# A reordered opening, rotary swaps on the sync engine's queue, and the first output panel's chunks among the attention's last steps

## The reference

```python
mk = rms_norm(rms_norm(mem) @ w_kv[:, :256], per head)       # memory keys, both layers
mv = rms_norm(mem) @ w_kv[:, 256:]                           # memory values
h  = rms_norm(x, norm_mix)
z  = h @ w_in_att                                            # keys, queries, memory queries, values
q, k = rope(rms_norm(q, per head)), rope(rms_norm(k, per head))
o  = concat(sink_softmax(q k^T, window 128) v, softmax(qx mk^T) mv)
x  = x + o @ w_out[0]                                        # the output projection
x  = x + relu(rms_norm(x) @ w_up)^2 @ w_down                 # MLP, then layer 1 in the same way
```

## Time and profile before

| | |
|---|---|
| time, median of 3 runs | 1163.68 us (1163.21 to 1164.44) |
| the profiled execution's own time | 1165.16 us |
| its span | 1163.4 us |
| mean granted TensorE clock | 0.996 of 2.4 GHz |
| TensorE matmuls busy | 1143.0 us, 98% of the span |
| VectorE, ScalarE, GpSimd busy | 781.8, 533.0, 130.4 us |

### The profile page before, as it was taken

How to read it: one execution, slowest core, us unless ns; L and a number is a source line. 1 busy time by engine, 2 the same in 40 slices (tenths; PEclk the granted TensorE clock), 3 DMA queues, 4 the chain that set the end, 5 groups by cost and what they waited for, 6 DMA issues and landing times.

```text
span 1163.4 us, 22291 instructions
## 1 busy us (share of the span) xinstructions
PE 1143.0 (98%) x9026; PEld 1103.2 (95%) x9026; DVE 781.8 (67%) x1215; ACT 533.0 (46%) x920; POOL 130.4 (11%) x143
## 2 busy tenths in 40 slices
PE   7999999999999999999999999999999999999998
PEld 7899646999999999999999999999999999999998
DVE  5857776798568468568657545689866856756853
ACT  6743886367137227326434222436713722732630
POOL 0018853000000000000240131200000000000000
PEclk8999999999999999999999999999999999999999
DMA  8553231213313222312522321221321331231241
GB/s 309 203 162 119 61 139 61 92 59 124 107 39 112 106 72 102 115 51 94 214 75 73 146 82 66 73 100 56 135 99 48 110 109 72 91 125 43 102 137 48
DMA packets 23866, 120.18 MB, mean 103 GB/s; under 512 B 2788, under 2 KB 7012, under 8 KB 10740
## 3 DMA queue, kind: packets, MB, share of 16 engines
q1 hardware_dynamic: 18612, 100.93, 24.8%
q0 software_dynamic: 1632, 10.54, 2.4%
q10 hardware_dynamic: 3552, 7.74, 2.0%
HBM read 111.29 MB, written 5.69 MB: 101 GB/s over the span
## 4 chain that ended last, share of the span: by engine, by line
PE 88%; DVE 3%; POOL 3%; ACT 2%; issue 2%; DMA 1%; ACTq 1%; SPq 0%; DVEq 0%; POOLq 0%
PE zps L507 48%; PE zps L801 25%; PE ops L801 4%; PE zps L789 4%; POOL sm L1955 2%; PE ops L699 1%; PE tps L671 1%; ACTq L1750 1%; PE zps L545 1%; PE zps L625 1%; ACT w_hi L1445 1%; DMA memx<-memT 1%; DMA tmp<-z 1%; ACT act_hi L1445 0%; DVE sm L1090 0%
## 5 line engine op out<-in xcount | busy, mean ns | idle before, releaser
L507 PE MATMUL zps<-act_hi,w_hi 128*128 128x272 f32 x1664 | 349.2, 291 | 0.0
L507 PE MATMUL zps<-act_hi,w_lo 128*128 128x272 f32 x1664 | 344.3, 288 | 0.0
L507 PE MATMUL zps<-act_lo,w_hi 128*128 128x272 f32 x1664 | 343.5, 288 | 0.0
L801 PE MATMUL zps<-xf,wf 128*128 128x272 f32 x2304 | 297.0, 288 | 0.0
L801 PEld LDWEIGHTS zps<-xf,wf 128*128 128x128 f32 x2304 | 292.2, 188 | 0.8
L507 PEld LDWEIGHTS zps<-act_hi,w_hi 128*128 128x128 f32 x1664 | 262.6, 189 | 4.4 <-issue 2.9
L507 PEld LDWEIGHTS zps<-act_lo,w_hi 128*128 128x128 f32 x1664 | 261.9, 189 | 0.0
L507 PEld LDWEIGHTS zps<-act_hi,w_lo 128*128 128x128 f32 x1664 | 260.1, 189 | 0.0
L1445 ACT ACTIVATE w_hi<-w_stage 128x2048 fp32r<-128x2048 f32 (+2 forms) x65 | 115.6, 1779 | 161.6 <-PE zps L507 122.8
L952 DVE TENSOR_TENSOR w_lo<-w_stage,w_hi 128x2048 fp32r<-128x2048 f32 x57 | 133.4, 2341 | 50.9 <-ACT w_hi L1445 50.6
L1445 ACT ACTIVATE wf<-w_sum 128x1024 fp32r<-128x1024 f32 x64 | 68.0, 1062 | 195.4 <-DVE w_sum L970 90.7
(11 more groups left out here) (193 smaller groups left out, 1279.9 us busy)
## 6 DMA issues: line engine op xcount, KB each, us to landing
w_stage<-wst SPq DMA_DIRECT2D x91, 1024.0 KB, 4.9
kx<-xkT POOLq DMA_DIRECT2D x4, 1024.0 KB, 8.5
vx<-xv POOLq DMA_DIRECT2D x4, 1024.0 KB, 7.4
x_res<-xT ACTq DMA_DIRECT2D x2, 1088.0 KB, 8.3
tmp<-z ACTq DMA_DIRECT2D x32, 68.0 KB, 2.1
yT<-x_res ACTq DMA_DIRECT2D x7, 272.0 KB, 2.0
memx<-memT SPq DMA_DIRECT2D x4, 256.0 KB, 5.2
w_stage<-wst SPq DMA_DIRECT2D x4, 256.0 KB, 5.4
```

What stands on the lines that cost most here:

```text
L507: mm = pe.matmul(zps[slot][:, h, 0:n], w_[:, d, k, w:w + 128], r_[:, k, c0 + h * n:c0 + (h + 1) * n], start=(j == 0 and i == 0), stop=(j = ...
L801: mm = pe.matmul(bank, wf_hl[pw][:, fw, a, :], x_form(l, px, fx, a)[:, 0, :], start=(begin and a == 0 and j == 0), stop=(a == KC // 2 - 1 ...
```

## The change

On ScalarE and VectorE the opening's instructions stand in another order. The first weight half of the memory's second column block is loaded in two DMAs with their own semaphores. The column sum stands after chunk 1 of panel 1, the last two turn_keys one panel later. The rotary swaps move from ScalarE's queue to SP's, among the weight loads, which are written out for it. Row 7 is rotated by VectorE; GpSimd rotates seven rows and clears its query tiles afterwards. In the attention VectorE makes the low parts of step J_SS + 1 before a pair's maxima. Panel 0 of the output projection is cut into its chunks: five stand in loop steps 14 to 16 of the attention, three after it.

```diff
 SP
-            sp.dma_start(stage[:, 1], wst[1]).then_inc(w_in[1], 16)
+            for h in range(2):
+                c = slice(4 * h, 4 * h + 4)
+                sp.dma_start(stage[:, 1, c], wst[1, :, c]).then_inc(w_in[1] if h else ld["w3"], 16)
...
             sp.dma_start(o_vs.rearrange("b s d -> s b d"), vb[ST:128, :, :]).then_inc(win_out, 16)
-            weights(Q_ATT + 2, Q_OUT0 + 1)
+            swapped(0)
+            weight(Q_ATT + 2, 0)
+            swapped(1)
+            swapped(2)
+            weight(Q_ATT + 2, 1)
+            swapped(3)
+            swapped(4)
+            weight(Q_OUT0, 0)
+            swapped(5)
+            swapped(6)
+            swapped(7)
+            weight(Q_OUT0, 1)
 TensorE
-                    pe.wait_ge(r_out, 5 if j == 0 else 8)
+                    pe.wait_ge(r_out, 5 if j == 0 else 7)
+                    if j:
+                        pe.wait_ge(r_last, 1)
...
+            def out_chunk(k):
+                if k == 0:
+                    pe.wait_ge(w_los[0], Q_OUT0 + 1)
+                    pe.wait_ge(z_free[0], Q_OUT0 * 2)
+                    pe.wait_ge(g_max, PAIR0[G_L1])
+                pe.wait_ge(g_olo, O0_READY[k])
+                hi, lo = act_hl[0]
+                for i, (w_, r_) in enumerate(((w_hi, hi), (w_hi, lo), (w_lo, hi))):
+                    for h in range(2):
+                        mm = pe.matmul(zps[0][:, h, 0:HALF], w_[:, 0, k, 0:128], r_[:, k, h * HALF:(h + 1) * HALF],
+                                       start=(k == 0 and i == 0), stop=(k == KC - 1 and i == 2))
+                if k == KC - 1:
+                    mm.then_inc(z_full[0], 1)
             def attention_0():
                 for j in range(1, G_L1 + 3):
                     for p in range(3):
+                        if j >= G_L1 and p < (2, 2, 1)[j - G_L1]:
+                            out_chunk(2 * (j - G_L1) + p)
...
-                panel(Q_ATT + i // 4, i % 4, *act_hl[0], ready=normed(0) if i == 0 else None)
-                if i == 0:
-                    colsum(2, NT)
-                if i in (1, 2):
-                    turn_keys(1 + i)
+                panel(Q_ATT + i // 4, i % 4, *act_hl[0], ready=normed(0) if i == 0 else None,
+                      between=(lambda k, mm: colsum(2, NT) if k == 1 else None) if i == 1 else None)
+                if i in (2, 3):
+                    turn_keys(i)
 VectorE
+            def rotate_last():
+                z, other = z0[:, 7, :], tmp[:, 5, :]
+                dve.wait_ge(r_sw[1], 64 * 4)
+                dve.tensor_tensor(z, z, cs[:, 0, :], ALU.mult)
+                link(dve.tensor_tensor(other, other, cs[:, 1, :], ALU.mult))
+                dve.tensor_tensor(z, z, other, ALU.add).then_inc(r_last, 1)
...
-                        if p == (0 if j - 4 >= J_LAST - 1 else 1) and 0 <= j - 4 < G_L1:
+                        if p == (0 if j - 4 >= J_LAST - 1 or j - 4 == J_SS + 1 else 1) and 0 <= j - 4 < G_L1:
...
             split_lo_halves(1, 0)
+            norm_lo(0, 0, 0)
             for m in range(2):
                 key_sums(m)
             split_lo(1, 1)
+            for k in range(1, 4):
+                norm_lo(0, k, 0)
             for m in range(2):
                 key_norm(m)
-            for k in range(4):
-                norm_lo(0, k, 0)
             split_lo(2, 0)
+            for k in (1, 2):
+                add_x0(k)
             for k in range(4, KC):
                 norm_lo(0, k, 0)
+            for k in range(3, KC):
+                add_x0(k)
+            split_lo(2, 1)
             for m in (2, 3):
                 key_sums(m)
-            for k in range(1, KC):
-                add_x0(k)
             for m in (2, 3):
                 key_norm(m)
-            split_lo(2, 1)
...
+                if i == 11:
+                    rotate_last()
                 take_scaled(q, p, z0[:, i, :])
 ScalarE
+            act.wait_ge(ld["x"], 16)
+            norm_hi(0, 0, 0)
             split_hi(1, 1)
+            for k in range(1, 4):
+                norm_hi(0, k, 0)
             root_keys(0)
             root_keys(1)
             take_memory(0, 2)
             take_memory(0, 3)
-            act.wait_ge(ld["x"], 16)
-            for k in range(4):
-                norm_hi(0, k, 0)
             take_memory(1, 0)
...
             take_memory(1, 2)
+            for k in range(3):
+                square_x0(k)
             act.wait_ge(ld["x1"], 16)
-            for k in (4, 5):
-                norm_hi(0, k, 0)
-            for k in (0, 1):
-                square_x0(k)
-            for k in (6, 7):
+            for k in range(4, KC):
                 norm_hi(0, k, 0)
             take_memory(1, 3)
-            for k in range(2, KC):
+            for k in range(3, KC):
                 square_x0(k)
+            split_hi(2, 1)
             keys_out(0)
             keys_out(1)
             root_keys(2)
             root_keys(3)
-            split_hi(2, 1)
...
-                if 2 <= i <= 9:
-                    swapped(i - 2)
 GpSimd
-            for r in range(8):
-                if r == 7:
-                    pool.wait_ge(n_ms, N_QX[0] + 2)
-                    pool.memset(qs[:, :, :, :], 0.0)
-                    link(pool.memset(qpad0[:, :, :, :], 0.0))
+            for r in range(7):
...
-            pool.wait_ge(r_out, 8)
+            pool.wait_ge(n_ms, N_QX[0] + 2)
+            pool.memset(qs[:, :, :, :], 0.0)
+            link(pool.memset(qpad0[:, :, :, :], 0.0))
             pool.wait_ge(ld["kt"], 16)
+            pool.wait_ge(r_out, 7)
```

More of the change, by code:

```diff
@@ L166, in build_kernel @@
         z_free = [sem(f"z_free{s}") for s in range(2)]
-        ld = {n: sem("ld_" + n) for n in ("con", "con2", "mem0", "mem1", "mem2", "mem3", "w0", "w1", "w2", "x", "x1", "rope", "kt", "vb", "kx0", "kx1", "vx0", "vx1")}
+        ld = {n: sem("ld_" + n) for n in ("con", "con2", "mem0", "mem1", "mem2", "mem3", "w0", "w1", "w2", "w3", "x", "x1", "rope", "kt", "vb", "kx0", "kx1", "vx0", "vx1")}
         m_hi, m_sq, m_los = sem("m_hi"), sem("m_sq"), [sem(f"m_lo{l}") for l in range(2)]
@@ L174, in build_kernel @@
         n_sq, n_ms, n_inv, n_inv2, n_dev, n_out = (sem("n_" + s) for s in ("sq", "ms", "inv", "inv2", "dev", "out"))
-        r_sw, r_out = [sem(f"r_sw{i}") for i in range(2)], sem("r_out")
+        r_sw, r_out, r_last = [sem(f"r_sw{i}") for i in range(2)], sem("r_out"), sem("r_last")
         v_t, v_out = sem("v_t"), sem("v_out")
@@ L455, in _, with swapped, weight @@
                 sp.dma_start(stage[:, 0, c], wst[0, :, c]).then_inc(ld[f"w{i}"] if i < 3 else w_in[0], 16)
-            sp.dma_start(stage[:, 1], wst[1]).then_inc(w_in[1], 16)
+            for h in range(2):
+                c = slice(4 * h, 4 * h + 4)
+                sp.dma_start(stage[:, 1, c], wst[1, :, c]).then_inc(w_in[1] if h else ld["w3"], 16)
+            def swapped(r):
+                sp.wait_ge(n_out, r + 1)
+                if r >= 2:
+                    sp.wait_ge(r_out, r - 1)
+                for to in range(0, 128, 32):
+                    sp.dma_start(tmp[to:to + 32, 4 + r % 2, :], z0[to ^ 32:(to ^ 32) + 32, r, :]).then_inc(r_sw[r % 2], 16)
+            def weight(q, d):
+                sp.wait_ge(w_los[d], q)
+                sp.dma_start(stage[:, d], wst[2 * q + d]).then_inc(w_in[d], 16)
             def weights(q0, q1):
@@ L776, in out_proj @@
                 for m in range(8):
-                    if m == 0:
+                    if m == 0 and l == 0:
+                        for k in (5, 6, 7):
+                            out_chunk(k)
+                    elif m == 0:
                         panel(q0, 0, *act_hl[l], ready=ready, order=order)
@@ L907, in _ @@
             attention_0()
-            out_proj(Q_OUT0, 0, lambda k: (g_olo, O0_READY[k]), range(KC))
+            out_proj(Q_OUT0, 0, None, None)
             mlp(Q_MLP0, 0, 3)
@@ L1743, in _ @@
             act.dma_start(con[:, 0:C_IDENT], cst[:, 0:C_IDENT]).then_inc(ld["con"], 16)
-            def swapped(r):
-                act.wait_ge(n_out, r + 1)
-                if r >= 2:
-                    act.wait_ge(r_out, r - 1)
-                for to in range(0, 128, 32):
-                    act.dma_start(tmp[to:to + 32, 4 + r % 2, :], z0[to ^ 32:(to ^ 32) + 32, r, :]).then_inc(r_sw[r % 2], 16)
             def take_memory(l, p):
@@ L1800, in _ @@
                     act.activation(msq[:, k, :], memx[:, k, :], ACT.Square).then_inc(m_sq, 1)
+            act.wait_ge(ld["w3"], 16)
+            copy(w_hi[:, 1, 0:4], stage[:, 1, 0:4]).then_inc(w_his_half, 1)
             act.wait_ge(w_in[1], 16)
-            copy(w_hi[:, 1, 0:4], stage[:, 1, 0:4]).then_inc(w_his_half, 1)
             copy(w_hi[:, 1, 4:8], stage[:, 1, 4:8]).then_inc(w_his[1], 1)
@@ L1849, in _ @@
                     split_next(Q_ATT + i // 4, i % 4)
-                if i in (1, 2):
-                    keys_out(1 + i)
+                if i in (2, 3):
+                    keys_out(i)
                 if i == 0:
@@ L1994, in _ @@
```

(2 more changed lines are left out.)

## The result

The changed kernel took 1168.83 us (median of 15 runs, 1166.63 to 1172.07), the kernel before 1165.02 beside it (15 runs): a ratio of 1.0037, 95% interval 1.0025 to 1.0048, so 4.3 us slower (3.8 by the two medians). The forecast was "no measurable change" at 1164.5. The number of the slower rival was met; of its mechanism only the first half was. The profiled execution took 1167.91 us by its own time, with a span of 1166.1 against 1163.4: 2.7 us can be placed step by step. The remainder goes with the clock of other executions and is taken up after the experiments.

The account below looks back on a forecast made before the run. TensorE was taken as the bound almost everywhere, with holes only in the opening and attention. Terms +0.8 + 1.4 + 1.2 - 0.9 - 0.7 - 1.0 = +0.8 us on 1163.68 gave 1164.5, range 1160.6 to 1167.9.

Parts of the forecast that it names:

- the slower rival: SP's queue: row 0's swaps stick behind o_vs, weight (4,0) issued only after; stall 4.8 to 6.6, 1167.4 to 1169.2; chance 0.27.
- Opening, the chain: Before the first head sum: longer chain starts the reciprocal at 52.35, not 51.55; +0.8 us (0.6 to 1.1).
- Opening, the clock: After some 4 us of TensorE idle, the low-clock stretch falls on panel 2 instead of panel 1; +1.4 us.
- SP's queue, the weight: Before the seventh head sum: weight (4,0) lands at 94.6 + s, stall 1.9 against 0.70; +1.2 us.
- s: Sum of the opening's two shifts, chain and clock, by which later times move; about 2.2 us.
- The rotations: Start of the attention: seven GpSimd rotations end near 127 + s, row 7 fits VectorE's wait; -0.9 us (0 to -1.6).
- The low parts and the chunks: Attention: low parts before maxima, -0.7 (0 to -0.9); five output chunks fill holes at the last turns, -1.0 (0 to -1.6).
- The sum: Whole kernel: all terms together, +0.8 us on the median of three, 1163.68, giving 1164.5.

Follow-up runs that it names:

- eight profiles: The changed kernel, unaltered, profiled eight times: the first profile and seven repeats; six of the repeats took 1165.46 to 1168.37 us.
- experiment 2: Changed kernel with the whole opening of before (orders, column sum, key turns, half weight loaded whole); 1161.67 us, 0.9977 of the kernel before.
- experiment 3: Changed kernel, last two key sums ahead of weight (2,1)'s low part, their norms, roots and copies behind panel 0's scaling and square; 1163.86 us, 0.9991.
- experiment 6: Changed kernel, o_vs on ScalarE's queue, first key norms ahead of norm low parts, reciprocal, scaling and square ahead of weight (2,1)'s low part; 1159.9 us, 0.9955.
- experiment 4: Kernel before with only the output panel's first five chunks moved into the attention's last three steps; 1164.09 us, 0.9995.
- experiment 9: Kernel before with only the low parts of step J_SS + 1 taken ahead of a pair's maxima; 1163.95 us, 0.9994.
- Experiment 8: Kernel before with only the new opening, swaps staying on ScalarE's queue; 1170.33 us, 1.0055.
- experiment 1: Changed kernel, only the copy o_vs moved from SyncE's queue to ScalarE's, issued in its second panel step; 1164.9 us, 0.9995 of the kernel before.
- experiment 7: Kernel before with only the swaps on SyncE's queue, seven rotations on GpSimd and row 7 on VectorE; 1165.38 us, 1.0001.
- experiment 10: Kernel before with the new opening and o_vs on ScalarE's queue, swaps staying there too; 1167.51 us, 1.0026.

## Why the forecast was wrong, step by step

**Opening, the chain: right.** Forecast +0.8 (0.6 to 1.1) with the reciprocal at 52.35; measured 52.98, and the first head sum 1.44 later. But 0.32 of that stands before the first key turn, where executions differ anyway; without it the chain is 1.12 longer. The forecast's stations fit when 0.32 is taken off: weight (2,0)'s low part ended at 39.61 (39.1 forecast), the last addition at 47.87 (47.3). The forecast overlooked that panel 0 itself needs that low part and now waits 0.35 us for it, ahead of the 0.5 us for the last addition.

**Opening, the clock: right.** Forecast +1.4, measured +1.56, in a stretch near 0.5 on panel 2 in all eight profiles. Experiments 2, 3 and 6, with less waiting in front of panel 2, have it at the full clock.

**SP's queue, the weight: the landing right by luck, the stall too large.** Forecast: landing at 94.6 + s, with s = 2.2 at 96.8; the split started at 97.11 on it. The forecast had the weight issued behind o_vs with a slow landing, as before; in fact it was issued only at 90.83, when the swap was out, as the slower rival had it, and landed 6.3 us later. TensorE itself was 3.23 us later there, not 2.2, and from split to head sum it took 5.7, so the stall was 0.94 and the step +0.23 instead of +1.2. The stall is 0.58 to 1.37 in the eight profiles, under the forecast's 1.9 in each; the 0.70 that it is counted against is missing in the profiles of experiments 4 and 9, which have the opening and the swaps of before. Experiment 8 shows the full size of the mechanism, 2.4 us.

**The rotations: the step that failed.** The forecast put row 7 into a wait of VectorE of 2.78 us ("three operations of about 0.75 fit there") and had the attention start 0.9 us sooner; it came 1.13 later, 2.0 us off. What row 7 itself waits for was not followed: its swap needs the buffer of row 5, which GpSimd leaves at 126.56, then four issues on SP and a landing, to 131.46. On GpSimd the seven rotations ended at 131.00, where 127 + s gave 129.2, and the memsets and copies behind them took 5.45 us, not 4.5. Both waits follow from a first swap at 93.6; with it at 80 to 82 (experiments 1, 2 and 7) neither occurs. The forecast had that swap at 92.5 + s = 94.7, so it knew the delay and missed what it does to row 7. VectorE's own rotation was not stretched beside GpSimd's copies: its three operations took 0.73 each.

**The low parts and the chunks: right.** Forecast -0.7 and -1.0; the low parts' longest wait fell by 0.8, and the end of the attention by 1.07 in experiment 4. Together with the smaller waits behind GpSimd's scaling the attention gave back 2.12.

**The sum.** By the profiles the sum is +2.5 at the MLP's start and +2.7 at the end, against +0.8. The forecast counted from 1163.68, a median of three; beside the changed kernel the kernel before took 1165.02, so 1.3 of the 4.3 us between 1164.5 and 1168.83 are the starting point, 1.9 the steps, and some 1.1 are left. What the forecast did not have at all is that executions of one kernel differ in where the clock falls. At 0.997 the changed kernel took 1166.63 to 1167.11 us, at 0.991 1170.97 to 1172.07. Its mean over 15 executions is 0.9942, that of before 0.9960 over the 31 beside experiments 1 to 4: 0.0018 of 1166 us is 2.1 us of TensorE time at most, and the profiled execution, at 0.996, shows little of it. Apart from the last few us, a stretch of low clock lost 1.7 us or 3.4 in the profiles; by that, as an estimate, an execution at 0.991 lost 10.5 us, six times 1.7, and the profiled ones two or three times. The kernels with fewer holes have higher means (0.9970, 0.9971, 0.9982 in experiments 2, 3 and 6) and gained more over their executions than their profiles place. Where the clock falls in the executions at 0.991 to 0.994 stays open; the start of the attention, the memory panels, and panel 2 (a longer fall, seen in experiment 1 alone) are places where profiles differ.

**The rivals.** The slower rival's number, 1167.4 to 1169.2, holds the result, but its place, a stall of 4.8 us or more before the seventh head sum, had 0.94. Its first half was right: the swaps did stick behind o_vs and the weight was issued only after them, though at 90.83 and not at 92.5 + s = 94.7. Its price fell on the rotations, and the number was met with the help of the starting point and the clock: that part is luck.

## What to carry to other kernels

When work moves to another engine, follow what its input waits for, buffers and queue included, and not only whether the engine has idle time there. A long copy in front of short, urgent transfers on one queue delays all of them; issued from another queue early enough to be through before they come, the same copy cost nothing that could be measured here. A hole in TensorE's work can have a second price behind it, in the clock, which one profile may show and the next may not: in experiment 1 the executions gained 4.9 us where the waits showed 2.3. And before two timelines are subtracted, look for a row that the change cannot touch: here it differed by 0.32 us between the two profiles, and by up to 1.9 between profiles of one kernel.

## What the hardware showed that was not expected

The granted clock fell behind one and the same hole in some executions and not in others: behind 1.66 us in experiment 4 (0.76 over the window above) and in experiment 7, not behind 1.64 in the profile of before, nor behind 1.66 and 1.80 in those of experiments 10 and 8.

Four issues of small transfers on SyncE took 13.41 us when a copy of 992 rows stood ahead of them on its queue, and 2.92 when it had gone; the engine's next weight could not even be asked for until then.

GpSimd's rotations ran at 5.3 to 5.7 us each, single operations between 1.35 and 3.39 us in the changed kernel; the longest stood beside a low part on VectorE that took 2.98 instead of 2.29.
